# Expert weights in loads of 2 MB into five landing buffers, in place of loads of 1 MB into ten

## What is computed

```python
# per token: one group of four, in it the top 2 of 8 experts (32 experts in all)
def expert_block(args):
    xb, e = args
    h = jax.nn.silu(xb @ w_gate[e]) * (xb @ w_up[e])    # w_gate, w_up: [1024, 512]
    return h @ w_down[e]                                # w_down: [512, 1024]
# x = x + sum over a token's two experts of gate_weight * expert output
```

## Time and profile before

| | us |
|---|---|
| Median of 3 runs | 1952.87 |
| Lowest and highest | 1949.64, 1952.91 |
| Profiled execution | 1956.59 |
| Its span in the profile | 1954.8 |
| TensorE busy in the span | 1815.3 (93%) |
| VectorE busy | 783.5 (40%) |
| ScalarE busy | 589.7 (30%) |
| Moved by DMA | 329.70 MB, mean 169 GB/s |

### The profile page before, as it was taken

How to read it: one execution, slowest core, us unless ns; L and a number is a source line. 1 busy time by engine, 2 the same in 40 slices (tenths; PEclk the granted TensorE clock), 3 DMA queues, 4 the chain that set the end, 5 groups by cost and what they waited for, 6 DMA issues and landing times.

```text
span 1954.8 us, 20262 instructions
## 1 busy us (share of the span) xinstructions
PE 1815.3 (93%) x8538; PEld 1325.7 (68%) x8538; DVE 783.5 (40%) x1014; ACT 589.7 (30%) x866; POOL 144.0 (7%) x105
## 2 busy tenths in 40 slices
PE   7998888796999999999889999999977989999997
PEld 6777776686554544543368888887855778888885
DVE  4666766544122232222243323324565343323333
ACT  4556344523211111111042212223334332212221
POOL 0001333202000000000000000000153000000000
PEclk9999999896999999999999999999998999999998
DMA  5312222442699999999932323232310042323221
GB/s 185 97 55 66 86 75 92 150 176 82 258 385 418 418 422 420 420 419 421 400 108 68 112 94 102 86 103 87 108 65 1 10 164 65 118 90 100 91 77 54
DMA packets 92401, 329.70 MB, mean 169 GB/s; under 512 B 6016, under 2 KB 15504, under 8 KB 67600
## 3 DMA queue, kind: packets, MB, share of 16 engines
q1 hardware_dynamic: 88208, 317.87, 43.0%
q0 software_dynamic: 1792, 6.26, 1.0%
q10 hardware_dynamic: 2304, 4.20, 0.6%
HBM read 322.01 MB, written 6.29 MB: 168 GB/s over the span
## 4 chain that ended last, share of the span: by engine, by line
PE 71%; DVE 5%; ACT 3%; DMA 2%; issue 1%; SPq 0%; DVEq 0%
PE PS L1125 10%; PE PS L1208 9%; PE PS L1210 9%; PE PS L1209 9%; PE PS L1204 6%; PE PS L1206 6%; PE PS L1205 6%; PE PS L1148 5%; PE PS L1158 2%; PE PS L1088 2%; PE PS L1089 2%; PE PS L1159 1%; DMA raw<-in_w_up_experts 1%; DMA rawz<-in_w_up_experts 1%; PE PS L1433 1%
## 5 line engine op out<-in xcount | busy, mean ns | idle before, releaser
L1838 DVE TENSOR_TENSOR lo<-raw,hi 128x2048 fp32r<-128x2048 f32 (+2 forms) x108 | 232.6, 2154 | 482.8 <-ACT hi L1499 482.7
L1499 ACT CAST hi<-raw 128x2048 fp32r<-128x2048 f32 (+2 forms) x110 | 197.6, 1799 | 387.0 <-PE PS L1206 202.3
L1208 PE MATMUL PS<-xh_ffn,hi 128*128 128x512 f32 x704 | 274.7, 390 | 5.8 <-DVE xl_ffn L1857 5.8
L1210 PE MATMUL PS<-xh_ffn,lo 128*128 128x512 f32 x704 | 274.6, 390 | 0.0
L1209 PE MATMUL PS<-xl_ffn,hi 128*128 128x512 f32 x704 | 274.4, 390 | 0.0
L1208 PEld LDWEIGHTS PS<-xh_ffn,hi 128*128 128x128 f32 x704 | 132.6, 188 | 33.8 <-issue 6.2
L1209 PEld LDWEIGHTS PS<-xl_ffn,hi 128*128 128x128 f32 x704 | 132.6, 188 | 27.6
L1210 PEld LDWEIGHTS PS<-xh_ffn,lo 128*128 128x128 f32 x704 | 132.4, 188 | 27.6
L1125 PE MATMUL PS<-raw,XG 128*64 128x512 f32 x416 | 138.1, 593 | 4.9 <-DMA raw<-in_w_up_experts 2.7
L1204 PE MATMUL PS<-hi,th_ffn 128*128 128x512 f32 x352 | 136.9, 389 | 0.0
L1205 PE MATMUL PS<-lo,th_ffn 128*128 128x512 f32 x352 | 136.9, 389 | 0.0
(11 more groups left out here) (388 smaller groups left out, 2991.7 us busy)
## 6 DMA issues: line engine op xcount, KB each, us to landing
raw<-in_w_in SPq DMA_DIRECT2D x26, 1024.0 KB, 5.1
raw<-in_w_gate_experts SPq DMA_DIRECT2D x26, 1024.0 KB, 12.6
raw<-in_w_up_experts SPq DMA_DIRECT2D x26, 1024.0 KB, 13.9
rawz<-in_w_up_experts SPq DMA_DIRECT2D x26, 1024.0 KB, 11.0
rawz<-in_w_down_experts SPq DMA_DIRECT2D x26, 1024.0 KB, 10.7
raw<-in_w_down_experts SPq DMA_DIRECT2D x25, 1024.0 KB, 10.0
rawz<-in_w_gate_experts SPq DMA_DIRECT2D x24, 1024.0 KB, 12.9
raw<-in_ffn_w_gate SPq DMA_DIRECT2D x16, 1024.0 KB, 5.1
```

Of the source, the lines that this page charges most:

```text
L1208: e.matmul(o, h[:, kk, c], xh[:, k, :], start=s0, stop=False)
L1210: x = e.matmul(o, l[:, kk, c], xh[:, k, :], start=False, stop=s1)
L1499: e.copy(q.hi[:, 0:w], q.raw[:, 0:w]).then_inc(*a_hi(u))
L1838: e.tensor_tensor(q.lo[:, 0:c], q.raw[:, 0:c], q.hi[:, 0:c].bitcast(F32), ALU.subtract).then_inc(*v_lo(u))
```

## The change

A unit is now a whole matrix of one expert: 2 MB, of which each partition gets 16 KB that lie in one piece in HBM. A product has two units, a pair of experts six. There are five landing buffers of 16 KB for each partition: four are the region of 64 KB (big[0] to big[3], each over two of the former buffers), the fifth (big[4]) lies at 127.84 KB of the remaining memory. The order of use is big[4], big[1], big[0], big[2], big[3]. Unit j takes the buffer of unit j - 5. TensorE signals only the end of a whole product. The first units wait for the last users of both former buffers under them, so big[2] and big[3] both wait for the last product of w_out. Small tiles make room: n2b, OU, WE, SG, HF and HT move to the region at 21 to 29 KB where rawx was. The semaphores of the expert loads are separate from those of the dense stages. The first four raw buffers of the FFN wait for units 92 and 91 of the experts (the up and gate products of pair 15), and its hi and lo buffers for the last down product.

```diff
@@ make_plan_moe
     for i in range(NP):
-        for kind, name in (("g", "w_gate_experts"), ("u", "w_up_experts")):
-            for h in range(2):
-                for q in range(2):
-                    w = I[name][0, 2 * i + q].rearrange("(p k) n -> p k n", k=8)
-                    plan.append(Unit((kind, i, h), w[:, 4 * h:4 * h + 4, :], 4, FF))
-        for h in range(2):
+        for kind, name, k in (("g", "w_gate_experts", 8), ("u", "w_up_experts", 8), ("d", "w_down_experts", 4)):
             for q in range(2):
-                w = I["w_down_experts"][0, 2 * i + q].rearrange("(p k) n -> p k n", k=4)
-                plan.append(Unit(("d", i, h), w[:, 2 * h:2 * h + 2, :], 2, D))
+                plan.append(Unit((kind, i), I[name][0, 2 * i + q].rearrange("(p k) n -> p k n", k=k), k, 4096 // k))
@@ buffers
-        rawx = at("rawx", 21, [128, 2048])
-        rawy = at("rawy", 134, [128, 2048])
-        rawz = [nc.alloc_sbuf_tensor_at(f"rawz{i}", [128, 2048], F32, offset=ring + (4 + i) * 8 * KB) for i in range(4)]
+        big = [nc.alloc_sbuf_tensor_at(f"big{i}", [128, 4096], F32, offset=ring + i * 16 * KB) for i in range(4)]
+        big.append(at("big4", 127.84375, [128, 4096]))
...
-        n2b = at("n2b", 128, [128, D])
+        n2b = at("n2b", 21, [128, D])
...
-        OU = at("OU", 133, [128, 256], F32R)
+        OU = at("OU", 28, [128, 256], F32R)
...
-        WE = at("WE", 132, [128, 256])
+        WE = at("WE", 27, [128, 256])
...
-        SG, HF, HT = (at(n, 124 + 2 * i, [128, 4, 128]) for i, n in enumerate(("SG", "HF", "HT")))
+        SG, HF, HT = (at(n, 21 + 2 * i, [128, 4, 128]) for i, n in enumerate(("SG", "HF", "HT")))
@@ what each buffer waits for
-        moe_raw = [raw[3], rawx, rawy, *raw[0:3], *rawz]
-        moe_first = [hg_done + z_done, hg_done, hg_done + z_done + [(v_hg, ("aTl", 3))], *r1, h1[0], h1[1], h1[0], h1[1]]
+        done_bh = [(v_ev, ("m", 1, 3)), (v_hg, ("aTl", 3))]
+        order = [big[4], big[1], big[0], big[2], big[3]]
+        moe_first = [hg_done + z_done + done_bh, hg_done + z_done + r1[2], r1[0] + r1[1], h1[0] + h1[1], h1[0] + h1[1]]
         for j, u in enumerate(p2):
-            u.slot = j % 10
-            u.raw = moe_raw[u.slot]
-            u.raw_free = moe_first[j] if j < 10 else [p2[j - 10].done]
-        r2 = ends(first_moe, len(p2), 10, lambda u: [U[u].done])
-        place(first3, len(p3), raw, hi, lo, [r2[3], r2[4], r2[5], r2[0]], [r2[6] + r2[8], r2[7] + r2[9]])
+            u.slot = j % 5
+            u.raw = order[u.slot]
+            u.raw_free = moe_first[j] if j < 5 else [p2[j - 5].done]
+        r2 = ends(first_moe, len(p2), 5, lambda u: [U[u].done])
+        place(first3, len(p3), raw, hi, lo, [r2[2], r2[2], r2[1], r2[1]], [r2[3] + r2[4], r2[3] + r2[4]])
@@ TensorE, gate and up product (the down product likewise)
-                w = loaded(kind, i, h)
+                w = loaded(kind, i)
                 for kk in range(4):
                     k = 4 * h + kk
                     for q in range(2):
                         s = 128 * (i % GP) + 64 * q
                         x = e.matmul(PS[64 * q:64 * q + 64, b, :], XG[(i // GP) % 2][:, k, s:s + 64],
-                                     w[q][:, kk * 512:kk * 512 + 512], start=k == 0, stop=k == 7)
-                x.then_inc(*m.p((kind, i, h)))
+                                     w[q][:, k * 512:k * 512 + 512], start=k == 0, stop=k == 7)
+                if h:
+                    x.then_inc(*m.p((kind, i)))
```

More of the change, by code:

```diff
@@ L735, in program @@
         d_x = [sig(f"d_x{i}", 16) for i in range(NB)]
-        d_w = [sig(f"d_w{i}", 16) for i in range(10)]
+        d_w = [sig(f"d_w{i}", 16) for i in range(4)]
+        d_big = [sig(f"d_big{i}", 16) for i in range(5)]
         d_z = [sig(f"d_z{i}", 16) for i in range(2)]
@@ L752, in __init__ @@
                 self.loop = loop
-                self.w = [sig(f"{n}d_w{i}", 16) for i in range(10)] if loop else d_w
+                self.w = [sig(f"{n}d_big{i}", 16) for i in range(5)] if loop else d_big
                 self.p, self.a, self.v = sig(n + "p_moe"), sig(n + "a_moe"), sig(n + "v_moe")
@@ L812, in program @@
         for u in p1 + p3 + p4 + p5:
-            u.slot = moe_raw.index(u.raw)
+            u.slot = raw.index(u.raw)
         before, experts, experts_again, after = [], [], [], []
@@ L913, in sp_program @@
                     sp.wait_ge(s, k)
-                load(u, d_w)
+                load(u, d_w if u < first_moe else d_big)
             yield
@@ L932, in sp_again @@
                 u = first_moe + j
-                if j >= 10:
-                    sp.wait_ge(again.p, p2[j - 10].key)
+                if j >= 5:
+                    sp.wait_ge(again.p, p2[j - 5].key)
                 dst = q.raw[:, 0:q.kc * q.n].rearrange("p (k n) -> p k n", k=q.kc)
@@ L1012, in m2_load @@
             def m2_load():
-                pool.wait_ge(main.p, ("d", NP - 1, 1))
+                pool.wait_ge(main.p, ("d", NP - 1))
                 e.dma_start(QW[:, 0, :], I["q_norm_2"].partition_broadcast(128)[:, 0, :]).then_inc(*d_b(0))
@@ L1107, in slots_, with loaded @@
                 freed[b2] = [(m.v, ("ws", i, 1))]
-            def loaded(kind, i, h):
-                u = first_moe + 12 * i + {"g": 0, "u": 4, "d": 8}[kind] + 2 * h
+            def loaded(kind, i):
+                u = first_moe + 6 * i + {"g": 0, "u": 2, "d": 4}[kind]
                 for q in range(2):
@@ L1141, in down @@
                 taken(b + 1)
[L1142 to L1150, removed]
+                w = loaded("d", i)
+                for j in range(4):
+                    for c in range(2):
+                        for q in range(2):
+                            x = e.matmul(PS[64 * q:64 * q + 64, b + c, :], HT[:, j, 64 * q:64 * q + 64],
+                                         w[q][:, j * D + c * 512:j * D + c * 512 + 512], start=j == 0, stop=j == 3)
+                x.then_inc(*m.p(("d", i)))
                 for c in range(2):
@@ L1458, in cols @@
                 if g >= 2:
-                    act.wait_ge(m.p, ("u", GP * (g - 1) - 1, 1))
+                    act.wait_ge(m.p, ("u", GP * (g - 1) - 1))
                 e.copy(XG[g % 2][:, c, :], PS[:, b, :]).then_inc(*m.a(("XG", g, c)))
@@ L1468, in hidden @@
             def hidden(i, bg, bu):
-                act.wait_ge(m.p, ("g", i, 1))
+                act.wait_ge(m.p, ("g", i))
                 if i:
@@ L1476, in turn_h @@
                 if i:
-                    act.wait_ge(m.p, ("d", i - 1, 1))
+                    act.wait_ge(m.p, ("d", i - 1))
                 e.copy(HT[:, :, :].rearrange("p j f -> p (j f)"), PS[:, b, :]).then_inc(*m.a(("HT", i)))
@@ L1483, in down @@
                     act.wait_ge(m.p, ("back", i - 1, 3, 1))
-                act.wait_ge(m.p, ("d", i, 1))
+                act.wait_ge(m.p, ("d", i))
                 for h in range(2):
@@ L1808, in hidden @@
                 dve.wait_ge(m.a, ("SG", i))
-                dve.wait_ge(m.p, ("u", i, 1))
+                dve.wait_ge(m.p, ("u", i))
                 if i:
```

## The result

| | before | changed |
|---|---|---|
| Median of the runs, us | 1952.32 (4 runs, 1949.64 to 1952.91) | 1974.74 (4 runs, 1971.55 to 1977.46) |
| Ratio, 95% interval | | 1.0115 (1.0103 to 1.0127) |
| Profiled execution, us | 1956.59 | 1977.46 |
| Its span, us | 1954.8 | 1975.6 |

The change costs 22.4 us. Slower was forecast, by a wait that did come, but by 13 us, with a range up to 1973 us; the time lies above it.

The account below looks back on a forecast made before the run. TensorE was taken to set the pace up to pair 11, DMA from pair 12. Ten waits plus a DMA-limited end gave +8.9 to +17.3 us, taken as +13: 1965.9 us from 1952.87, range 1959 to 1973.

Parts of the forecast that it names:

- ten waits in pairs 2 to 11: Ahead of these up products TensorE waits for the second up unit: 7.7 us landing against 6.87 us of gate product.
- the DMA-limited end: From pair 12's second up unit, 19 units in a full queue, then 19.1 us to the last eviction; ending near 988.
- Rivals 1 to 3: Whole kernel: 1 no change within 0.2%, 6 in 100; 2 faster, 3 in 100; 3 much slower, 6 in 100.
- no change: Expert stage: a 2 MB load lands in 6.7 us, no pair waits, +1.2 us, 1954 us; 6 in 100.
- a slow DMA: Expert stage: 16 KB pieces run slower than 8 KB ones; at 389 GB/s +36 us, 1989 us; 6 in 100.
- an end without gaps: Long pieces speed up the DMA-bound end, TensorE without gaps after 890; at most down to 1945.6 us; 3 in 100.
- Rival 4: Expert loads: pieces are cut to 8 KB anyway, the ring stays five; +12.3 us, within the forecast, no separate chance.
- The start of the stage: First expert loads wait for the last w_out product but land by 460, with 40 us of cover: no cost.
- the line from 2 KB and 8 KB pieces: Per-engine times of 89.8 and 311.3 ns, extended to 607 ns for 16 KB: 432 GB/s, 4.85 us for 2 MB.
- a fixed part that grows with the piece: Fixed part of a load's landing: 2.2 us with 2 KB pieces, 2.56 with 8 KB, carried on to 3.0 with 16 KB.
- the wait of 0.7 to 1.3 us in each pair: TensorE's stop ahead of the up products of pairs 2 to 12 until a w_up load lands.
- the case of 432 GB/s and 3.0 us fixed: 2 MB load with higher rate and longer fixed part: 1.1 us wait per pair, stage ending at 988.3, +13.4 us.

Follow-up runs that it names:

- the filled kernels: Changed kernel plus small unread products ahead of up products where TensorE waits: in pairs 2 to 15, 1977.19 us; only in pairs 13 to 15, 1974.74 us.
- the second trace: The changed kernel run once more, nothing altered, for another profile: 1978.02 us, 1.0127 of the kernel before.

## Why the prediction was wrong, step by step

**Right.** The second up unit waits for the end of the down product, and TensorE for that unit: ten waits in pairs 2 to 11, then the DMA-limited end. The shares came as listed: 400 to 401 GB/s and a DMA share of 0.96 where 403 to 411 was said, a period of 31.2 to 31.5 in nine of ten periods where 30.6 to 31.2 was said. Rivals 1 to 3 fell: neither no change, nor a slow DMA (428 GB/s where it limits), nor an end without gaps. Rival 4 fell too: the packets are 16 KB. The start of the stage had its cover: its first gate product waited for no load.

**The 16 KB load.** Forecast 432 GB/s and 3.0 us fixed, landing 7.85. Measured 428 (4.90 us for 2 MB) and landings of 7.7 to 8.0 in nine of the ten middle pairs of the first trace, 9.4 in the tenth. Of the rate that the line from 2 KB and 8 KB pieces promised (421 to 432), two thirds came. The landing came out right, but partly by luck: the prediction took it from a fixed part that grows with the piece, for a load alone in the queue. Pieces of 8 KB in the same ring land in 7.5 to 8.0 us, nearly as late, and the windows show that 2.7 MB are moved until a load of 2.1 MB is there. So the growth with the piece is not shown, and the sharing with the next load, which no term held, is. The Trainium skill's fit, 2.0 us plus the bytes over 436 GB/s ("DMA: Bandwidth & Descriptors", section "Anatomy of one DMA — SWDGE (gpsimd) path"), gives 6.8 us: 1 us under the shortest landing.

**The step that failed: the wait of 0.7 to 1.3 us in each pair, taken as the whole price of the wait, and the same in each pair.** The ordinary wait was about right (1.18 us ahead of the up product at 568.42). But a stopped TensorE pays more than the wait, and not every landing is the ordinary one. Against the case of 432 GB/s and 3.0 us fixed (+13.4), the first trace has:

| term | forecast us | measured us |
|---|---|---|
| ten periods, waits (0.1 us longer each) | 11.0 | 11.7 |
| ten periods, restart: up product 7.09 in place of 6.86 | 0 | 2.3 |
| one late landing with the lower clock, 34.53 against 31.4 | 0 | 3.1 |
| end: last up product at the lower clock, 9.88 in place of 6.87 | 0 | 3.0 |
| end: last up weights, 97.6 us after issue in place of 95.2 | 2.4 | 4.7 |
| sum | 13.4 | 24.8 |

The first four rows are read from the chain. In the last, 19 units at 4.90 us explain 0.9 of the 2.3. The rest has the size of the sharing seen above:

```profile
877.00:974.55 97.55, 85.01 (x380) 34.93 (x376) 23.20 (x35) 9.21 (x15) 0.00 (x0) 0.98 1.00 420
```

In these 97.55 us 41.0 MB were moved, and the 19 units are 39.8 MB: 1.1 MB belong to others, of which some 0.6 MB lie in the ordinary landing too. The other 0.5 MB take an estimated 1.3 us. No experiment changed the order of the loads, so this part is argued from the windows alone.

That the lower clock makes the long up products is shown by the filled kernels. What it costs the end is less than the 3.0 of the table: with the clock up, the end was only 1.9 us shorter (117.8 us), still 3.5 over the 114.3 that the forecast had (3.0 + 92.2 + 19.1). The 24.8 of the stage are also one trace; the second has 28.1, and the medians differ by 22.4.

The range was too narrow because it took in only the two unknowns of the load, and treated a wait as its length. Its upper bound had neither restart, nor clock, nor the scatter of landings. Yet waits of about 3 us in pairs 13 to 15 followed from its own numbers: six units take 29.1 us, and TensorE would need 25.7.

**The cause was the ring.** 8 KB pieces in the same ring are as slow, half the combination put where TensorE waited brings back 11.6 us, and four places cost 93 more. What counts is how long one step takes to land, against the work that runs between the release of its place and the need. Eight places of 1 MB, released by halves, lose less than half of what five of 2 MB lose.

## What to carry to other kernels

In a ring of buffers, find for each load the event that frees its place and the moment that its data are needed, and compare the work between them with the landing time of that load. Count in what is issued close behind it. The total of bytes under way does not answer this alone: eight places of 1 MB cost 10 us here and five of 2 MB 22, though with one size of step fewer places cost more each time. The fewer and larger loads raised the rate by 1.7% where DMA limits, and took 7.9 us to land where one of 1 MB took 5.1. Price a new wait of TensorE above its length: the restart (0.2 us here), the lower clock when it is long, and late landings, which a ring without margin passes on in full.

## What the runs showed of the hardware

- Loads with pieces of 16 KB to a partition run at 428 GB/s in a full queue, those with pieces of 8 KB at 421 (end of the changed kernel against the same ring with 8 KB pieces, and the earlier trace rows).
- One 2 MB load into a nearly empty queue, with the next load issued 0.4 us behind it, took 7.7 to 8.5 us in 26 of 30 cases and 8.6 to 9.9 in four. Until it was there, 2.6 to 2.9 MB were moved in the ordinary cases and 3.0 to 3.5 MB in the late ones.
- A chain of 32 float32 products takes 6.87 us right behind another such chain, 7.02 after other products and 7.09 after a wait.
- After waits of 2.0 us (gate product at 891.98 with half the combination between), 2.4 us (823.72 in the second trace) and 2.7 us and more, the next product mostly took 8.4 to 10.1 us in place of 7.1, at a granted clock of 0.50 to 0.77 for its first microseconds. After waits of 2.4 us (693.71 with 8 KB pieces) and 3.2 us (791.12 in the second trace) it took 7.09 at a clock of 1.00.
